# Gated linear attention outputs in longer runs of one tile shape, and two moves in the down projection

## The reference

```python
kv_chunk = jnp.einsum('bnshd,bnshv->bnhdv', kc * jnp.exp(b_last[:, :, None] - bc), vc)
o_intra = jnp.einsum('bnhts,bnshv->bnthv', scores, vc)
o_inter = jnp.einsum('bnthd,nbhdv->bnthv', qc * jnp.exp(bc), s_start)
o = (o_intra + o_inter).reshape(B, T, H, DV)
...
a, g = jnp.split(u, 2, axis=-1)
return (a * jax.nn.silu(g)) @ w_down
```

## Time and profile before

| what | value |
|---|---|
| median of 3 runs | 960.11 us (959.9 to 960.29) |
| profiled execution, its own time | 959.88 us |
| its span in the trace | 958.1 us |
| PE busy | 940.3 us, 98% of the span |
| DVE busy | 687.0 us, 72% |
| ACT busy | 477.4 us, 50% |
| POOL busy | 470.5 us, 49% |
| chain that ended last | PE 75%, DVE 15%, issue 3% |

### The profile page before, as it was taken

The page is one execution under the profiler, slowest core; times in us unless marked ns, Lnnn a source line. Parts: engine busy times, 40 slices in busy tenths (PEclk is TensorE's granted clock), DMA queues, the critical chain, the costliest instruction groups (busy, mean ns, idle before and its releaser), DMA issues.

```text
span 958.1 us, 19041 instructions
## 1 busy us (share of the span) xinstructions
PE 940.3 (98%) x7447; PEld 854.6 (89%) x7447; DVE 687.0 (72%) x1239; ACT 477.4 (50%) x750; POOL 470.5 (49%) x355
## 2 busy tenths in 40 slices
PE   6999999999999999999999999999999999999997
PEld 5799899977788889999987999999999999778886
DVE  6508358962576669544945998777777778999996
ACT  5244165523766664342324376555555556565460
POOL 1386733223423326773632558899999887100003
PEclk9999999999999999999999999999999999999999
DMA  9896231226101114688761204678887322446571
GB/s 338 271 159 101 68 88 46 68 67 187 34 24 45 45 44 146 201 264 282 262 205 44 80 10 133 167 211 218 219 211 181 94 84 76 150 154 232 185 263 66
DMA packets 134243, 137.03 MB, mean 143 GB/s; under 512 B 8870, under 2 KB 105099, under 8 KB 133899
## 3 DMA queue, kind: packets, MB, share of 16 engines
q1 hardware_dynamic: 127592, 125.50, 41.8%
q0 software_dynamic: 4688, 9.01, 6.2%
q10 hardware_dynamic: 1875, 1.32, 0.4%
HBM read 124.51 MB, written 10.24 MB: 141 GB/s over the span
## 4 chain that ended last, share of the span: by engine, by line
PE 75%; DVE 15%; issue 3%; SPq 2%; POOL 1%; ACT 1%; DMA 1%; DVEq 0%; ACTq 0%; POOLq 0%
PE PA L1810 7%; PE PA L1811 6%; PE PA L1812 6%; PE PJ L1086 6%; PE PJ L1091 5%; PE PJ L1087 5%; DVE d_far L3359 2%; DVE d_near L3353 2%; PE PJ L1604 2%; PE PA L1530 2%; PE PJ L1605 2%; PE PJ L1609 2%; SPq L603 2%; PE PJ L1810 2%; PE PJ L1811 2%
## 5 line engine op out<-in xcount | busy, mean ns | idle before, releaser
L862 POOL TENSOR_TENSOR wlo<-wraw,whi 128x1024 fp32r<-128x1024 f32 x32 | 81.4, 2547 | 168.0 <-ACT whi L1941 167.8
L1086 PE MATMUL PJ<-h_hi,whi 128*128 128x320 f32 x336 | 104.7, 320 | 0.1
L1087 PE MATMUL PJ<-h_lo,whi 128*128 128x320 f32 x336 | 101.1, 309 | 0.0
L1941 ACT ACTIVATE whi<-wraw 128x1024 fp32r<-128x1024 f32 x39 | 41.0, 1052 | 71.4 <-PE PJ L1091 23.3
L1091 PE MATMUL PJ<-h_hi,wlo 128*128 128x320 f32 x336 | 76.5, 309 | 0.0
L1086 PEld LDWEIGHTS PJ<-h_hi,whi 128*128 128x128 f32 x336 | 63.0, 188 | 5.8 <-issue 3.6
L1063 POOL TENSOR_TENSOR x<-x,d_raw 128x512 f32<-128x512 f32 x2 | 2.6, 1298 | 128.2 <-DVE d_raw L3520 128.2
L1029 POOL TENSOR_TENSOR behind<-behind_val,behind 128x512 fp32r<-128x512 f32 x40 | 59.9, 1497 | 10.1 <-ACT behind L2436 10.1
L1087 PEld LDWEIGHTS PJ<-h_lo,whi 128*128 128x128 f32 x336 | 63.1, 188 | 0.0
L2465 ACT ACTIVATE d_hi<-d_raw 128x1024 fp32r<-128x1024 f32 x44 | 45.3, 1055 | 33.4 <-DMA d_raw<-in_w_down_dram 18.8
L1812 PE MATMUL PA<-h_hi,behind 128*128 128x320 f32 x192 | 59.3, 309 | 0.0
(11 more groups left out here) (640 smaller groups left out, 3353.1 us busy)
## 6 DMA issues: line engine op xcount, KB each, us to landing
wraw<-in_w_in_dram SPq DMA_DIRECT2D x72, 256.0 KB, 3.2
d_raw<-in_w_down_dram SPq DMA_DIRECT2D x33, 512.0 KB, 4.3
ada_rest<-in_w_ada_dram SPq DMA_DIRECT2D x32, 512.0 KB, 6.2
wraw<-in_w_up_dram SPq DMA_DIRECT2D x48, 256.0 KB, 4.7
raw_even<-in_w_up_dram SPq DMA_DIRECT2D x40, 256.0 KB, 4.4
ada<-in_w_ada_dram SPq DMA_DIRECT2D x16, 512.0 KB, 7.5
d_ahead<-in_w_down_dram SPq DMA_DIRECT2D x11, 512.0 KB, 5.3
d_ahead<-in_w_down_dram POOLq DMA_DIRECT2D x11, 512.0 KB, 5.9
```

The lines of the kernel that those rows point to most:

```text
L862: pool.tensor_tensor(wlo[:, slot, 0:k, :], wraw[:, slot, 0:k, :], whi[:, slot, 0:k, :].bitcast(F32), ALU.subtract).then_inc(lo_done, done)
L1086: pe.matmul(out, whi[:, slot, w0 + k, :], hi(k)[:, tok], start=start and k == k0, stop=False)
L1087: pe.matmul(out, whi[:, slot, w0 + k, :], lo(k)[:, tok], start=False, stop=False)
L1941: act.activation(whi[:, slot, :, :], wraw[:, slot, :, :], ACT.Copy).then_inc(hi_done, done)
```

## The change

Three edits.

1. **Chunk outputs.** For each group of two tiles all products with `A` come first, then all carried ones; `qk_spread(0)` stands between the first and the second group. The numbers of products stay; only their order and the marks for the first and last product of a bank change.
2. **Far additions.** The two additions of line 3487 leave VectorE's second run. GpSimd does them in the tail, once the last sums' low part is made (`("sums", KH - 1)`). The two context additions move up one `k`, into the freed place.
3. **Combinations of k = 3, 4, 5.** `early_low(k - 1)`, `second_fourth(k)` and `first_of(k)` stand behind `far_low_units(k)` and no more ahead of `weight_low(k)`, as they did for k = 2 already. The table `PART_ORDER` that gives the semaphore counts follows.

```diff
+N_BEHIND = 6
...
-for k in range(3, KH):
+for k in range(2, N_BEHIND):
+    PART_ORDER += [("weight", k), ("rows", k), ("last", k), ("opened", k), ("early", k - 1), ("fourth", k)]
+for k in range(N_BEHIND, KH):
...
-MERGED = [("mult", 0), ("near", 0), ("mult", 1), ("near", 1), ("far", 0), ("far", 1), ("context", 0), ("context", 1)]
+MERGED = [("mult", 0), ("near", 0), ("mult", 1), ("near", 1), ("context", 0), ("context", 1)]
...
+            pool.wait_ge(actlo_set, PART_LOW["sums", KH - 1])
+            pool.wait_ge(ev_set, E_DOWN + 7)
+            for i in range(2):
+                x_ = as_rows(x2[:, i, BANK:D])
+                pool.tensor_tensor(x_, x_, kept(8, i), ALU.add).then_inc(pooled_set, 1)
...
+                if g == 1:
+                    qk_spread(0)
                 for t in range(t0, t0 + nt):
-                    if t == 1:
-                        qk_spread(0)
                     for dt in range(2):
                         for r in range(2):
...
-                                           start=True, stop=t == NT - 1)
+                                           start=t == t0 and dt == 0, stop=t == NT - 1 and dt == 1)
...
-                        for d in range(2 if t < NT - 1 else 0):
+                for t in range(t0, min(t0 + nt, NT - 1)):
+                    for dt in range(2):
+                        for d in range(2):
                             for r in range(2):
...
                 third(k)
-                if k > 2:
+                if k >= N_BEHIND:
                     early_low(k - 1)
                     second_fourth(k)
                     first_of(k)
...
                 far_low_units(k)
-                if k == 2:
-                    early_low(1)
-                    second_fourth(2)
-                    first_of(2)
+                if k < N_BEHIND:
+                    early_low(k - 1)
+                    second_fourth(k)
+                    first_of(k)
                 fourth_low(k)
...
-                if k < 6:
+                if k < 5:
                     merged(*MERGED[2 * (k - 2)])
                     merged(*MERGED[2 * (k - 2) + 1])
```

More of the change, by code:

```diff
@@ L113 @@
               ("early", 0)]
-PART_ORDER += [("weight", 2), ("rows", 2), ("last", 2), ("opened", 2), ("early", 1), ("fourth", 2)]
-for k in range(3, KH):
+for k in range(2, N_BEHIND):
+    PART_ORDER += [("weight", k), ("rows", k), ("last", k), ("opened", k), ("early", k - 1), ("fourth", k)]
+for k in range(N_BEHIND, KH):
     PART_ORDER += [("early", k - 1), ("weight", k), ("rows", k), ("last", k), ("opened", k), ("fourth", k)]
@@ L845, in _ @@
             for i in range(2):
-                sp.wait_ge(pooled_set, P_DOWN + 2 * i + 1)
+                sp.wait_ge(pooled_set, P_DOWN + 2 + 2 * i + 1)
                 y_out(i, 1)
             for i in range(2):
-                sp.wait_ge(pooled_set, P_DOWN + 4 + i + 1)
+                sp.wait_ge(pooled_set, P_DOWN + 6 + i + 1)
                 y_out(2 + i, 1)
-            sp.wait_ge(pooled_set, P_DOWN + 7)
+            sp.wait_ge(pooled_set, P_DOWN + 9)
             y_out(2, 0)
@@ L1062, in _ @@
                 x_ = x2[:, i, BANK:D]
+                pool.wait_ge(pooled_set, P_DOWN + i + 1)
                 pool.tensor_tensor(x_, x_, d_raw[1][:, i, :], ALU.add).then_inc(pooled_set, 1)
@@ L1068, in _ @@
                 x_ = x2[:, 2 + i, BANK:D]
-                pool.wait_ge(pooled_set, P_DOWN + 2 * i + 2)
+                pool.wait_ge(pooled_set, P_DOWN + 2 + 2 * i + 2)
                 pool.tensor_tensor(x_, x_, d_raw[0][:, 2 + i, :], ALU.add).then_inc(pooled_set, 1)
@@ L1429, in _ @@
                                                lvl[64 * r:64 * r + 64, d, dt, t * P:(t + 1) * P],
-                                               start=False, stop=d == 1)
+                                               start=False, stop=t == t0 + nt - 1 and dt == 1 and d == 1)
                                 if t == t0 + nt - 1 and dt == 1 and d == 1:
@@ L3483, in merged @@
                     dve.tensor_tensor(x2[:, i, 0:BANK], x2[:, i, 0:BANK], ev2[:, i, :], ALU.add).then_inc(y_set, 1)
[L3484 to L3487, removed]
                 else:
```

## The result

| what | before | after |
|---|---|---|
| median of 20 runs each, same chip | 960.15 us (959.37 to 960.56) | 962.12 us (959.85 to 963.21) |
| ratio, 95% interval | | 1.0018 (1.0011 to 1.0024) |
| profiled execution, its own time | 959.88 us | 962.27 us |
| its span, its mean granted clock | 958.1 us, 0.999 | 960.4 us, 0.998 |

The granted clock is TensorE's clock as a share of its full one: 1.00 is the upper of its two levels. The forecast was 960.4 us, 0.35 us more than before, and no change within 0.2%. The ratio says 0.18% slower, which is still inside that bound, but its interval leaves out 1: the change is a small loss and not level. The medians lie 1.97 us (0.21%) apart, and 962.12 us is 0.02 us beyond the range given and just inside the band called slower (above 962.0), which had a chance of 0.10.

A forecast was written before the change was run, and what follows sets the result against it. TensorE is busy 98%, but near the end VectorE's list sets the pace. The terms -2.4 - 0.4 + 3.15 = +0.35 us gave a median of 960.4 us, forecast as no change, range 957.7 to 962.1 us.

The forecast's parts named there:

- Edit 1, -2.4 us: TensorE's chunk outputs: twelve of 17 changes between array shapes go, at 0.20 us each, -2.4 us.
- an outcome of 0: Chunk outputs: by the skill's rule that weight loads are pulled ahead whatever their order, edit 1 would give 0.
- Edit 2, -0.4 us: VectorE's second run: list 1.2 us shorter, but the k = 7 weight sum waits for load data, so -0.4 us.
- Edit 3, +3.15 us: VectorE at k = 3 to 5: moved combinations no longer cover ScalarE's casts, delaying its list to the end by 3.15 us.
- its three pieces: VectorE's added delay from edit 3: 0.6 us at k = 3, some 1.95 at k = 4, 0.6 at k = 5.
- The cause at k = 4: ScalarE's weight casts stand behind the gate, which waits for line 3185; VectorE idles some 2.5 us.
- loses most at k = 6: TensorE's start at k = 6: the rows' low part that releases it comes 3.1 us later.
- VectorE's list goes on without idle time: Behind k = 6: no idle time, so the 3.15 us delay reaches the last far low part.
- Combinations cheap: Rival on edit 3: VectorE's idle time at k = 4 is filled or made good; 956.5 to 958.2 us, chance 0.17.
- shape changes free: Rival on chunk outputs: edit 1 gives nothing, 962.9 us; chance 0.11 together with VectorE later still.
- far additions full: Rival on edit 2: the load lands sooner and the full 1.2 us is gained, 959.7 us; no separate chance given.
- Slower: Whole kernel above 962.0 us, chance 0.10, drawn from free shape changes or VectorE later still.

The follow-up runs named there:

- e2: Edit 2 alone (two far additions to GpSimd, context additions one k earlier) on the kernel before: 959.92 us, ratio 0.9995.
- e4: Edits 1 and 2 without edit 3, on the kernel before: 957.32 us, ratio 0.9971.
- e1: Edit 1 alone (chunk outputs) on the kernel before: 957.84 us, ratio 0.9978.
- e8: e4 with the context additions left behind k = 5 of the second run, nothing behind k = 4: 956.10 us, ratio 0.9963.
- e5: Changed kernel with the combinations moved behind the far low part for k = 3 only: 958.31 us, ratio 0.9977.
- e6: Changed kernel with the combinations moved behind the far low part for k = 3 and 4 only: 960.32 us, ratio 1.0000.
- e7: Changed kernel with ScalarE's gate and first tap behind the two casts of k = 4, not in front: 959.38 us, ratio 0.9989.
- e10: e8 with ScalarE's gate behind the casts of k = 4, as in e7: 955.64 us, ratio 0.9955.
- e9: Changed kernel with surplus matmuls filling TensorE's pauses (6 in n = 3, 12 in n = 5 of the second half): 961.24 us, ratio 1.0012.
- e3: Edit 3 alone (combinations of k = 3 to 5 moved) on the kernel before: 963.96 us, ratio 1.0043.
- e11: e7 with 12 surplus matmuls in TensorE's pause in n = 5 of the second half: 958.68 us, ratio 0.9982.

## Why the prediction was right, and what it missed

- **Edit 1, -2.4 us.** Right to 0.1 us, in the rows (2.36) and alone on the chip (-2.42). The price per change of shape, 0.20 us, held for all twelve. The Trainium skill has a rule on either side. The one that the prediction weighed, on weight loads pulled ahead, led it to an outcome of 0, and that did not come. The other is in the Trainium skill's page "TensorEngine Tiling (Array Packing)", "Key Properties": changing the tiling mode drains TensorE. The measured 0.20 us agree with it; that it is a drain, the runs do not show.
- **Edit 2, -0.4 us.** The measured -0.34 agrees, though its interval takes in no change, and B gives 0.12 in e2 and 0.66 in e4 against e1. The cause was right. e8 shows it: with the far low part, and so the weight load behind it, 1.2 us earlier, VectorE's wait for the load is gone and B has the whole 1.2 us. The size hangs on when a load lands: the wait at k = 7 was 0.93 us in e2, 0.30 in e4, 0.99 in the changed kernel.
- **Edit 3, +3.15 us.** Right for VectorE's list, and right in its three pieces (e5, e6). The cause at k = 4, the gate in front of ScalarE's casts, is shown by e7 with e10: with the late gate k = 4 costs what its neighbours cost.
- **What was missed** is a term of the sum that was not there. The prediction said that TensorE "loses most at k = 6", where its start would be over 2 us late, and took this as a delay that VectorE's list had caused already. It did not ask what a pause of that length does to TensorE's clock. In 13 of 20 executions the clock fell; in the profiled one of them it was halved for 3.65 us behind the pause, 1.6 us were lost, and this came back into VectorE's list through ScalarE's cast. That is 962.1 for 960.4 us. The prediction also said that "VectorE's list goes on without idle time" behind k = 6. The trace of the kernel before has 0.51 us there (at 886.38 us), behind a cast that waits for TensorE, and that is where the loss came in.
- **Luck.** The sum of the three edits was right for the seven executions whose clock stayed up (960.46 us) and 2 us short for the other thirteen. Forecast were 0.35 us more, measured 1.97 in the medians. That this still came out at the edge of the range is luck: the range was made for other rivals, and the fall happened to be no larger.
- **The rivals.** "Combinations cheap" fell (A grows by 3.19), "shape changes free" fell (e1), "far additions full" did not happen in the changed kernel (a wait of 0.99 us for the load), but e8 brings it about.
- **Range and chances.** "Slower" rested on free changes of shape or a still later VectorE. The fall of the clock, 1.7 us more and so 962.1, should have stood there as a rival of its own.

Open: why the same pause halves the clock in some executions and not in others, and how long a pause may be before it does. By the Trainium skill, "TensorE: Matmul & The Clock Gate", section "What's actually happening", the monitor runs on by itself and does not start anew with a kernel, which would fit; no run here shows it. The kernel before has one execution at 0.998 as well (962.38 us), and its profile has no such pause, so a fall may have other causes. Why e9 as a whole is slower than its profile minus its late start, and the one long execution of e6, stay open too.

## What to carry to other kernels

Before work is moved behind the instruction it used to precede, ask what it covered: here 1.86 us of combinations hid ScalarE's casts, which stood behind a gate, so the move cost 3.2 us of VectorE's list. Putting the gate behind the casts gave back 2.4 us of it, and 1.0 us without the move. When a move makes a pause of TensorE longer, price the pause and a halved clock behind it, and look at the mean clock of every run, not only at the median. An addition that leaves an engine's list gives its time only if the transfers that hang on that list move up as well.

## What the runs showed of the hardware

- A pause of 2.2 to 2.4 us of TensorE was followed by a fall of the granted clock from 1.00 to about half in the profiles of the changed kernel and of e7; in that of e3 it was not. The changed kernel and e3 also have a pause of 1.6 us before k = 4, some 17 us earlier; e7 has no other wait of TensorE for VectorE in the down projection but the one of 0.8 us near the end. By the mean clock it fell in 13 of 20 executions of the changed kernel, 6 of 11 of e7 and 2 of 5 of e3. In the changed kernel the fall came 1.5 us after work had been taken up again, in e7 at once (the first matmuls behind the pause are slow already):

```profile
856.43 0.56 PE L1838 MATMUL PJ<-d_hi,a_hi 128*128 128x512 f32 x1 [2.22 <-DVE a_lo L3320]
856.79 0.63 PE L1839 MATMUL PJ<-d_near,a_hi 128*128 128x512 f32 x1
...
860.18 0.40 PE L1838 MATMUL PJ<-d_hi,c_hi 128*128 128x512 f32 x1
```

- With surplus matmuls in such a pause (12 of 512 columns, 2.7 us) the clock fell in none of 22 executions, and B was shorter by 1.36 us (e11 against e7) and 2.13 us (e9 against the changed kernel, where the pause before k = 4 was filled too). The medians fell by 0.7 and 0.9 us, to 0.3 and 0.8 us above the averages of the executions without a fall.
- A change between matrices of 128 rows and of 64 rows, either way, costs TensorE 0.20 us here, in runs of 4 steps (0.64 us instead of 0.44) as in runs of 16 (1.98 instead of 1.78).
